# A pre-norm factor that moves from in front of a layer's products to behind them

## What is computed

```
x  = rms_norm(x, final_g)                      # end of the first block
h  = rms_norm_2(x, g_pre)                      # the even layer
p  = h @ w_in
a_val, a_gate, z_a, q, k, v, o, z_b, gates = split_cols(p, EVEN_SIZES)
u  = a_val * sigmoid(a_gate);  u = depthwise_conv_centred(u, conv_w, conv_b)
y_a = silu(group_layer_norm(u, ...)) * silu(z_a)
hm = mlstm forward + mlstm backward, of q, k, v and the gates, by head
hm = sigmoid(o) * rms_norm_2(hm, hn_g)
y_b = hm * silu(z_b)
x  = x + rms_norm_2(concatenate([y_a, y_b]) @ w_out, g_post)
```

## Time and profile before

| | us |
|---|---|
| median of three runs | 845.76 |
| the three runs | 845.69 to 846.05 |
| the profiled execution, as timed | 846.07 |
| its span, first to last instruction | 844.2 |
| TensorE busy | 834.4 (99% of the span) |
| VectorE busy | 565.7 (67%) |
| ScalarE busy | 498.7 (59%) |

### The profile page before, as it was taken

The page is one execution under the profiler, slowest core; times in us unless marked ns, Lnnn a source line. Parts: engine busy times, 40 slices in busy tenths (PEclk is TensorE's granted clock), DMA queues, the critical chain, the costliest instruction groups (busy, mean ns, idle before and its releaser), DMA issues.

```text
span 844.2 us, 14306 instructions
## 1 busy us (share of the span) xinstructions
PE 834.4 (99%) x5548; PEld 741.6 (88%) x5548; DVE 565.7 (67%) x1048; ACT 498.7 (59%) x851; POOL 24.4 (3%) x30
## 2 busy tenths in 40 slices
PE   8999999999999999999999999999999999999997
PEld 7999898889878888888878799999998889999786
DVE  5443445876968777785776766367886585668765
ACT  6654456765466665664674335676666574665554
POOL 0000000002500000000000000000000001000000
PEclk9999999999999999999999999999999999999999
DMA  9654753325446555546535434434445644545311
GB/s 341 266 219 149 282 201 134 109 101 173 148 150 232 176 181 196 200 153 219 190 114 223 149 134 167 138 112 151 150 150 185 231 160 169 187 143 208 113 50 75
DMA packets 21694, 144.15 MB, mean 171 GB/s; under 512 B 2529, under 2 KB 3169, under 8 KB 4992
## 3 DMA queue, kind: packets, MB, share of 16 engines
q1 hardware_dynamic: 20736, 140.55, 46.5%
q10 hardware_dynamic: 896, 2.73, 0.9%
HBM read 142.22 MB, written 1.05 MB: 170 GB/s over the span
## 4 chain that ended last, share of the span: by engine, by line
PE 92%; DVE 3%; DMA 2%; ACT 2%; issue 0%; SPq 0%; POOL 0%; DVEq 0%; ACTq 0%
PE PS L464 90%; DMA ring<-w 1%; DVE wl L1967 1%; ACT wh L1368 1%; PE PS L864 0%; PE PS L1279 0%; DMA V<-gains 0%; PE PS L641 0%; ACT PB L1408 0%; ACT hx L1382 0%; DVE hx L2032 0%; PE PS L865 0%; PE PS L866 0%; DVE xb L2516 0%; DVE PB L2508 0%
## 5 line engine op out<-in xcount | busy, mean ns | idle before, releaser
L1967 DVE TENSOR_TENSOR wl<-ring,wh 128x1024 fp32r<-128x1024 f32 x248 | 305.4, 1236 | 203.9 <-ACT wh L1368 203.5
L464 PE MATMUL PS<-hx,wh 128*128 128x256 f32 (+1 forms) x2088 | 404.1, 304 | 0.6 <-DVE wl L1967 0.2
L1368 ACT ACTIVATE wh<-ring 128x1024 fp32r<-128x1024 f32 x248 | 261.4, 1058 | 218.4 <-PE PS L464 201.2
L464 PEld LDWEIGHTS PS<-hx,wh 128*128 128x128 f32 x2088 | 331.7, 191 | 15.7 <-issue 3.5
L464 PE MATMUL PS<-hx,wl 128*128 128x256 f32 x1212 | 288.7, 283 | 0.1
L464 PE MATMUL PS<-wh,hx 128*128 128x512 f32 (+2 forms) x896 | 233.0, 363 | 0.3 <-ACT wh L1368 0.3
L464 PEld LDWEIGHTS PS<-hx,wl 128*128 128x128 f32 x1212 | 211.1, 191 | 3.6 <-DVE wl L1967 0.3
L464 PEld LDWEIGHTS PS<-wh,hx 128*128 128x128 f32 x896 | 160.3, 189 | 27.2 <-issue 1.7
L464 PE MATMUL PS<-wl,hx 128*128 128x512 f32 (+2 forms) x448 | 141.6, 360 | 0.2
L464 PEld LDWEIGHTS PS<-wl,hx 128*128 128x128 f32 x448 | 84.3, 189 | 14.1 <-DVE wl L1967 1.6
L1654 ACT ACTIVATE T<-PS 128x512 f32<-128x512 f32 x22 | 13.2, 598 | 27.0 <-PE PS L464 27.0
(11 more groups left out here) (310 smaller groups left out, 679.8 us busy)
## 6 DMA issues: line engine op xcount, KB each, us to landing
ring<-w SPq DMA_DIRECT2D x127, 1024.0 KB, 4.8
cn<-consts SPq DMA_DIRECT2D x2, 1051.0 KB, 10.8
V<-gains ACTq DMA_DIRECT2D x3, 512.0 KB, 5.9
cn<-consts SPq DMA_DIRECT2D x1, 1050.5 KB, 9.5
xa<-x SPq DMA_DIRECT2D x2, 512.0 KB, 4.6
ring<-w SPq DMA_DIRECT2D x2, 512.0 KB, 6.2
out<-xb SPq DMA_DIRECT2D x4, 256.0 KB, 2.1
BIG<-rows SPq DMA_DIRECT2D x1, 448.0 KB, 10.4
```

The costliest lines, as they stand in the source:

```text
L464: return nc.tensor.matmul(o, lhsT, rhs, start=start, stop=stop, skip_group_check=True)
L1368: A(wh[:, q % SPLITS, :], ring[:, i % RING, e:e + HALF], ACT.Copy).then_inc(sem("hi_ready"), 1)
L1967: TTn(wl[:, q % SPLITS, :], ring[:, PLACE[unit_of(q)] % RING, e:e + HALF], wh[:, q % SPLITS, :].bitcast(F32), ALU.subtract).then_inc(sem(" ...
```

## The change

The even layer's rows are turned straight from `xa`, with no factor of the norm in them. The gain column `g3` takes `final_g` in (one small VectorE product at the start). The squares, roots and the inverse are computed while the first products of `conv_in` run. The factor of a row is then multiplied in behind the products: where tokens lie down the partitions, as the scale of ScalarE's evacuation (tanh of the gate, v; now one instruction for each row tile) or in the tables of the convolution (`conv_fwd`); where they lie along the columns (q, k, z_a, o, z), by a VectorE multiplication with `RROW`, a row of the factors that one more TensorE product spreads over the partitions. What ScalarE did straight from PSUM on z_a, o and z it now does in SBUF behind that multiplication.

```
@@ TensorE, norm_transposes @@
-                            pe.wait_ge(sem(f"rows_scaled[{t}]"), 2 * n + k // 4 + 1)
+                        if k % 4 == 0 and n == 2:
+                            pe.wait_ge(sem("x2_ready"), 1 if t == 0 else 2 + k // 4)
...
-                    if t == 0 and n == 2:
-                        idle_products(JOINT_WARM[n][1], TURNED[n][0])
@@ TensorE, behind the down projection @@
-            idle_products(JOINT_WARM[2][0], G[0])
+            norm_transposes(2)
             taps_turned(3)
-            norm_transposes(2)
             normed(2)
             for p in range(3):
                 if p == 1:
                     pe.wait_ge(sem("taps_kept"), 4)
                 conv_pair(p)
+                if p == 1:
+                    pe.wait_ge(sem("row_rstd"), 4)
+                    mm(PS[:, SC[0], 0:S], c("mean", P, 2 * P), PTS[:, 0, 0:S], True, True)\
+                        .then_inc(sem("rstd_spread"), 1)
@@ ScalarE: the squares and roots leave their place ahead of turned_evac @@
+            def v_evac(h):
+
+                u = v_unit(h)
+                for t in range(TT):
+                    ins = A(V[:, t, h * 256:(h + 1) * 256], bank_of(u)[:, t * S:(t + 1) * S], ACT.Copy, scale=r3[t])
+                freed(ins, u)
...
                         halves(half_at(u) + half + SPLITS)
+                        if n == 1:
+                            even_roots()
                         act.wait_ge(sem("half_used"), half_at(u) + half + 1)
-                        A(cols2(T1[:, n // 2 % 2, :]), PS[:, o:o + TT, S:2 * S], ACT.Tanh, scale=0.5)\
-                            .then_inc(sem("a_gate"), 1)
+                        if n == 1:
+                            act.wait_ge(sem("row_rstd"), 4)
+                        for t in range(TT):
+                            ins = A(T1[:, n // 2 % 2, t * S:(t + 1) * S], PS[:, o + t, S:2 * S], ACT.Tanh,
+                                    scale=half_r[t])
+                        ins.then_inc(sem("a_gate"), 1)
+                    if n == 0:
+                        even_squares(half)
                     multiplied(half_at(u) + half)
...
+                        if 12 <= n < 16:
                             i = n - 12
-                            freed(A(BIG[:, 2 * i:2 * i + 2, :], cols2(b), ACT.Silu), u)
+                            act.wait_ge(*read(u))
+                            A(BIG[:, 2 * i:2 * i + 2, :], BIG[:, 2 * i:2 * i + 2, :], ACT.Silu)
@@ ScalarE, even_evac @@
                 if kind == 0:
-                    freed(A(V[:, :, h * 256:(h + 1) * 256], cols2(bank_of(u)), ACT.Copy), u)
-                elif kind == 1:
-                    freed(A(BIG[:, 8 + 2 * h:10 + 2 * h, :], cols2(bank_of(u)), ACT.Tanh, scale=0.5), u)
+                    v_evac(h)
+                    return
+                act.wait_ge(*read(u))
+                if kind == 1:
+                    o = BIG[:, 8 + 2 * h:10 + 2 * h, :]
+                    A(o, o, ACT.Tanh, scale=0.5)
                 else:
                     if h:
                         act.wait_ge(sem("oz_ready"), h)
-                    A(T1[:, 1, :], bank_of(u), ACT.Tanh, scale=0.5).then_inc(sem("z_tanh"), 1)
+                    A(T1[:, 1, :], SM[:, h % 2, :], ACT.Tanh, scale=0.5).then_inc(sem("z_tanh"), 1)
@@ VectorE @@
+            def row_factors():
+
+                dve.wait_ge(sem("row_ssq[0]"), 3)
...
+                for t in range(TT):
+                    q = row_rstd(3, t)
+                    own(TS(half_r[t], q, 0.5, None, ALU.mult))
+                    f = c("conv_fwd", t * 2 * P, (t + 1) * 2 * P)
+                    dve.wait_ge(sem("taps_in"), 32)
+                    own(TS(f, f, q, None, ALU.mult))
+                    settled()
+                    TS(PTS[:, 0, t * P:(t + 1) * P], ident, q, None, ALU.mult).then_inc(sem("row_rstd"), 1)
...
             def conv_in(p):
 
                 halves(half_of("conv_in") + 4 * p + 3 + SPLITS)
+                if p == 0:
+                    row_factors()
...
+            def row_scaled(o, u):
+
+                dve.wait_ge(sem("half_used"), half_at(u) + 2)
+                dve.wait_ge(sem("rstd_rows"), 1)
+                freed(TTn(o, cols2(bank_of(u)), RROW.unsqueeze(1).broadcast_to([P, 2, S]), ALU.mult), u)
...
+                if i % 2 and i < 16:
+                    n = i // 2
+                    u = FIRST["qk"] + n
+                    o = QK[:, 2 * n:2 * n + 2, :] if n < 4 else BIG[:, 2 * n - 8:2 * n - 6, :]
+                    row_scaled(o, u)
...
+                if s_ == 21:
+                    z_scaled(3)
                 for kind, n in step_:
...
+                if s_ < EVEN_HALVES and s_ % 6 == 1:
+                    n = s_ // 6
+                    row_scaled(BIG[:, 8 + 2 * n:10 + 2 * n, :], o_unit(n))
                 if s_ < EVEN_HALVES and s_ % 6 == 3:
                     n = s_ // 6
-
-                    u = z_unit(n)
+                    z = SM[:, n % 2, :]
+                    if n < 3:
+                        z_scaled(n)
+                    dve.wait_ge(*read(z_unit(n)))
                     dve.wait_ge(sem("z_tanh"), n + 1)
```

More of the change, by code:

```diff
@@ L1670, in _, with even_squares, even_roots @@
                     A(ropes[1], ropes[1], ACT.Sin).then_inc(sem("rope_tables"), 1)
[L1671 to L1686, removed]
+            def even_squares(t):
+                if t == 0:
+                    root_table(2)
+                    act.wait_ge(sem("x2_ready"), 1)
+                    row_square(2, 0, cols2(xa[:, 0, :]))
+                    act.wait_ge(sem("gained"), 1)
+                    row_square(3, 0, cols2(xb[:, 0, :]))
+                    return
+                for h in range(2):
+                    c_ = slice(h * 512, (h + 1) * 512)
+                    act.wait_ge(sem("x2_ready"), h + 2)
+                    part_square(2, h, xa[:, 1, c_])
+                    act.wait_ge(sem("gained"), h + 2)
+                    act.wait_ge(sem("row_ssq[0]"), 4)
+                    part_square(3, h, xb[:, 1, c_])
+            def even_roots():
+                row_root(2, 0)
+                act.wait_ge(sem("row_bias"), 1)
+                row_root(3, 0, stat[:, 40:41])
+                part_root(2)
+                part_root(3)
             halves(half_of("conv_in") + 1)
@@ L2335, in _ @@
-            settled()
-            own(TS(stat[:, 46:47], stat[:, 46:47], EPS * EPS, None, ALU.add))
-            settled()
-            dve.wait_ge(sem("row_ssq[1]"), PARTS_DONE[2, 1])
-            STT(stat[:, 45:46], ssq[:, 5:6], EPS, stat[:, 46:47], ALU.mult, ALU.add).then_inc(sem("row_bias"), 1)
-            scaled(3, 1, xb)
-            turned_evac(2, "g3", half_of("conv_in"))
-            for t in range(TT):
-                q = row_rstd(2, t)
-                dve.wait_ge(sem("rows_scaled[%d]" % t), 6)
-                own(TS(xb[:, t, :], xb[:, t, :], q, None, ALU.mult))
+            turned_evac(2, "g3", half_of("conv_in"))
@@ new lines, in row_factors @@
+            def row_factors():
+                dve.wait_ge(sem("row_ssq[0]"), 3)
+                TS(stat[:, 40:41], ssq[:, 4:5], EPS, EPS * EPS, ALU.mult, ALU.add).then_inc(sem("row_bias"), 1)
+                part_bias(2)
+                dve.wait_ge(sem("row_ssq[1]"), PARTS_DONE[3, 0])
+                own(STT(stat[:, 46:47], stat[:, 42:43], EPS, stat[:, 43:44], ALU.mult, ALU.add))
+                settled()
+                own(TS(stat[:, 46:47], stat[:, 46:47], EPS * EPS, None, ALU.add))
+                settled()
+                dve.wait_ge(sem("row_ssq[1]"), PARTS_DONE[2, 1])
+                STT(stat[:, 45:46], ssq[:, 5:6], EPS, stat[:, 46:47], ALU.mult, ALU.add).then_inc(sem("row_bias"), 1)
+                for t in range(TT):
[4 more added lines that the diff above has]
+                    own(TS(f, f, q, None, ALU.mult))
+                    settled()
+                    TS(PTS[:, 0, t * P:(t + 1) * P], ident, q, None, ALU.mult).then_inc(sem("row_rstd"), 1)
+                for t in range(TT):
+                    q = row_rstd(2, t)
+                    own(TS(xb[:, t, :], xb[:, t, :], q, None, ALU.mult))
@@ L2393, in _ @@
                     dve.wait_ge(sem("small_done"), 2)
-                    own(TTn(gt2, cols2(PS[:, SC[0], 256:384])[:, :, 0:16],
-                            r("b_gate").unsqueeze(1).broadcast_to([P, TT, 16]), ALU.add))
+                    for t in range(TT):
+                        own(STT(gt2[:, t, :], PS[:, SC[0], 256 + 64 * t:272 + 64 * t], r3[t], r("b_gate"), ALU.mult,
+                                ALU.add))
                     settled()
@@ L2410, in _, with z_scaled @@
                     .then_inc(sem("lstm_rows_copied"), 1)
+            def z_scaled(n):
+                row_scaled(cols2(SM[:, n % 2, :]), z_unit(n))
             for s_, step_ in enumerate(EVEN_STEPS):
@@ L2904 @@
     put("g3", columns(a["even_g_pre_2"][0], 8))
+    put("g_final", columns(a["final_g"], 8))
     put("tap_b", columns(a["even_conv_b_2"][0], 8))
```

48 lines of the change are left out of this document (21 added, 27 removed).

## The result

| | before | after |
|---|---|---|
| median | 845.76 | 876.53 |
| all runs | 845.69 to 846.05 | 873.64 to 876.96 |
| span of the profiled execution | 844.2 | 874.9 |

The ratio is 1.0356, with a 95% interval of 1.0337 to 1.0376. The forecast was 868.6, with a range up to 875.5: the direction and the places were right, the size was not.

What follows compares the result with a forecast made beforehand. TensorE, busy 99% of the span, was taken as the bound. The profiled 846.07 + 1.6 (join) + 0.5 (q, k, z_a) + 19.0 (heads) + 1.7 (clock) = 868.9, so 868.6 for the median; range 862.0 to 875.5.

Steps and rivals of the forecast that it cites:

- The clock: TensorE's waits at "pv" in the heads: one fall to 1.2 GHz, +1.7, with ends 0 and 5.1 (three falls).
- The rival at 872.0: Heads 0 to 2: each leaves TensorE idle for 4 to 7, so three falls of the clock, 872.0; chance 0.17.
- The heads: Tanh of o and z and the copy to PTS wait for VectorE's multiplications: TensorE late by 19.0 in sum.
- the 0.2 for V's copy in two: Heads 1 to 3: 0.2 added to each head's lateness because V's copy is made in two.
- Head 3: Last head: z multiplied behind "yb", the copy to PTS at 634.0 against 632.35, 1.7 late and 0.2 for V.
- The join: Down projection to the new layer's first products: 2.7 gained, 4.3 paid, net +1.6, with ends -2.7 and +5.
- the early start: In the join: transposes need only `xa`, so the layer's first product starts at 433.9, 2.3 before 436.21.
- half 6: In the join: its weights `wl` come at 455.2, wanted at 452.7, so TensorE is 2.5 late.
- Multiplications of q, k, z_a, hidden: Eight VectorE multiplications of 0.69 fit VectorE's room; only the last `z_a` runs into the first decay: +0.5, between 0 and 0.8.
- All cover holds: Rival, faster: z's multiplication is early enough in every head and the join's squares hide on ScalarE, 843.1; chance 0.06.
- The waits don't add up: Rival, heads: engines catch up during one head's wait, so only the largest counts, 854.5 or some 852; chance 0.10.
- the early start doesn't come: Rival, join: the transposes still wait, so 2.3 to 2.7 are not gained and the payments stay, 871.3; chance 0.04.

Runs made afterwards that it cites:

- e3_squares_early: Changed kernel with ScalarE's table load and the first row tile's two squares put back ahead of the copies of the turned rows: 871.43.
- e11_z_alone: Changed kernel with the factor left out of o alone, z keeping its multiplication, in the changed kernel's order: 863.00.
- e4_copy_first: Changed kernel with ScalarE's copy to PTS moved ahead of the tanh of z: 860.93.
- e1_heads_no_factor: Changed kernel with the factor left out of o and z, ScalarE taking both tanh straight from PSUM, all else as changed: 848.39.
- e12_o_alone: Changed kernel with the factor left out of z alone, o keeping its multiplication, in the changed kernel's order: 857.57.
- e7_o_late_too: e6_z_behind_square with the tanh of o a step later, behind the next weights, and VectorE's multiplication of o ahead of yb: 849.46.
- e8_all: e7_o_late_too and e3_squares_early together: 846.02, ratio 0.9991 to 1.0009 against the kernel before.
- e6_z_behind_square: e4_copy_first with the tanh of z moved behind the square of the head's result, and VectorE's product with z behind the next head's decay: 855.66.
- e5_fill_short: Changed kernel with 8, 11 and 8 idle products ahead of TensorE's wait for PTS in heads 0 to 2: 869.59.
- e2_fill: Changed kernel with 15, 20 and 15 idle products ahead of TensorE's wait for PTS in heads 0 to 2: 875.55.

## Why the prediction was wrong

**The clock, the step that failed.** "I take one fall, +1.7": there were four, and they cost 9.0. The number of falls was the larger error. Three stood in heads 0 to 2, where a rival had them; the fourth, in the join behind a wait of 1.72, nothing in the prediction had. The row by which I priced the danger said that 2.4 of idling had sufficed at the end of the program, three of the waits I had reckoned myself were 4.2 to 7.1, and I still took one fall as the likeliest and gave three falls 0.17. The reason I wrote against it (half a wait is filled by products in between) had no row behind it. It fitted only the waits of 1.6 at o's bank, which I had counted inside; the others stood in one piece. The price was low too: 1.7 for each, where the heads had 2.2 to 2.7. It isn't a fixed one: e3_squares_early has the same three waits, and 30.19, 29.08 and 22.93 from one "pv" to the next, so its falls cost 1.5, 1.7 and 2.4. I took it from the program's start by setting 4.94 against fourteen times 0.25; but 0.25 was a length with the pipeline's fill in it, and 30 passes in a row show 0.22, so the start itself lost some 1.9. With 9.0 for the falls in place of 1.7 the sum would have been 875.9.

**The Trainium skill's rule on the clock** (TensorE: Matmul & The Clock Gate, HAM oscillation) would have given the better time: every wait of 3.4 to 5.3 that wasn't filled brought a fall, in after, e3_squares_early and e11_z_alone alike. Of the shorter ones most brought none (1.55 in after, 1.83 in e11_z_alone, 1.99 in e4_copy_first). The rival at 872.0, which went by the same count of falls, was priced too low as well. The Trainium skill's table load of 2.7 (ScalarE: Activation LUTs, What ACT_TABLE_LOAD costs) was not borne out here: at 449.86 and 437.20 the trace of after has 1.28 and the next instruction right behind; the idle 1.38 ahead of the load at 449.86 is a wait for VectorE's factors.

**The heads, right in size.** The sum was 19.0 against 18.1, head by head 4.2, 7.1, 5.8 and 1.9 against 4.0, 6.9, 5.5 and 1.8 (a bank's wait and that at PTS together). e11_z_alone confirms the chain with one link taken out. That the waits add up was right: they don't work each other off from head to head. That part of them would be a wait for o's bank I had not foreseen, and the 0.2 for V's copy in two has nothing in e1_heads_no_factor to show for it.

**Head 3, right number with a wrong name.** I wrote that z is multiplied behind "yb". The copy to PTS of that head stands ahead of the tanh of z; the multiplication behind "yb" is that of o. e12_o_alone keeps the wait of 1.78, e11_z_alone doesn't have it.

**The join, near enough.** Net +1.6 forecast, +1.0 in the trace without the clock and the head start of 0.35: the early start came as reckoned, half 6 was 1.7 late and not 2.5. e3_squares_early shows the lateness to be ScalarE's, and curable.

**Multiplications of q, k, z_a, hidden,** as said: what e1_heads_no_factor has over before is 2.6, no more than the 1.0 of the join, the 0.6 ahead of the decay and the 1.6 of the clock, which its profiled execution lost behind the wait of 1.69.

**The rivals.** "All cover holds" is what e7_o_late_too and e8_all bring about by another order; the change as made had none of it. "The waits don't add up" and "the early start doesn't come" are both refuted by the first table of waits and the rows of the join.

## What to carry to other kernels

When work moves from an engine with a copy to one that stands a few steps behind it, look at what the waiting instruction holds up in its own queue: here a tanh that nobody wanted soon stood ahead of a copy that TensorE wanted at once, and moving it behind that copy and the square that follows won 21 of 31 (in the profiled executions some 1.6 of this is the fall in the join, which came and went by itself). Follow every reordering to the next instruction in the same queue, since the wait moves there first (from the copy to the square), and look again for waits that it had hidden (o's bank: gone in e4_copy_first, back in e6_z_behind_square). And price each wait of a fast engine twice: its length, and the work at half the clock behind it, by the rows of the trace that show the clock falling.

## What the runs showed of the hardware

**A wait of 1.7 may or may not bring the clock down.** The same wait for half 6, in after (1.72) and in e6_z_behind_square (1.69), a microsecond each behind it:

```profile
455.00:456.00 1.00, 1.00 (x4) 0.81 (x3) 1.00 (x2) 0.00 (x0) 0.00 (x0) 0.50 0.00 0
```

```profile
455.00:456.00 1.00, 1.00 (x6) 0.82 (x5) 1.00 (x2) 0.12 (x1) 0.00 (x0) 1.00 0.00 0
```

At 0.50 in the first, 1.00 in the second, with the same work. Of the profiled executions with this wait three show the fall (after, e1_heads_no_factor, e4_copy_first) and six don't. The wait of 1.8 in head 3 brought a fall in e5_fill_short and e12_o_alone and none in after, e2_fill, e3_squares_early and e6_z_behind_square. Such a fall moves a run by 1.6 to 1.7. Runs of after lie 3.3 apart, those of before 0.4 (1.7 in a later series). That the falls make this scatter wasn't tested by itself, but the clock goes with the time: the run of 873.64 has a mean granted clock of 0.990, those of 876.9 have 0.986; of e12_o_alone's runs the two at 856.8 and 856.9 have 0.999 and 1.000, the two at 858.3 and 858.9 have 0.997. What decides it in a given execution wasn't found.

**GpSimd's sum of the squares doesn't have one length.** The same instruction on 128x256 took 0.73 and 0.95 in heads 0 and 1 of after, where VectorE mostly stood idle beside it, and 1.73 in heads 0 to 2 of e4_copy_first, where VectorE ran products from SBUF to SBUF and `wl` at the same time. So the wait moved to this place cost a microsecond more than the length from a quiet stretch says. That VectorE's work beside it is the cause is not shown: in head 0 of e6_z_behind_square `wl` ran beside it as well, for 0.64, and it took 0.74. Lengths on GpSimd are rough in these profiles.
